# The last megabyte of a weight stream, moved as 114 and 14 partitions

## What is computed

```python
h = x + (merged @ p['w_o']).astype(x.dtype)
h = h + moe(rmsnorm(h, p['norm2_w']), ...)
# moe, for a block of tokens xblk of expert e:
gl = jnp.minimum(xblk @ w_gate[e] + b_gate[e], SWIGLU_LIMIT)
ul = jnp.clip(xblk @ w_up[e] + b_up[e], -SWIGLU_LIMIT, SWIGLU_LIMIT)
return ((ul + 1.0) * (gl * jax.nn.sigmoid(SWIGLU_ALPHA * gl))) @ w_down[e] + b_down[e]
...
y_prompt = rmsnorm(hp, final_norm_w)
y_sample = rmsnorm(hs, final_norm_w)
```

## Time and profile before

| | us |
|---|---|
| median of 3 runs | 1409.24 |
| lowest and highest | 1408.97, 1410.02 |
| the profiled execution, its own time | 1409.07 |
| its span, first to last instruction | 1407.3 |
| TensorE busy | 1340.0 (95%) |
| VectorE busy | 461.4 (33%) |
| ScalarE busy | 230.9 (16%) |
| DMA, mean over the span | 323 GB/s |

### The profile page before, as it was taken

One profiled execution on the slowest core, in us unless ns is written; L12 is line 12 of the kernel. 1 busy time (PEld: TensorE's weight loads), 2 busy tenths in 40 slices (PEclk: granted clock), 3 DMA queues, 4 the chain that ended last, 5 costly groups with the idle time before them and its releaser, 6 DMA issues.

```text
span 1407.3 us, 16551 instructions
## 1 busy us (share of the span) xinstructions
PE 1340.0 (95%) x7269; PEld 671.8 (48%) x7269; DVE 461.4 (33%) x866; ACT 230.9 (16%) x468; POOL 0.2 (0%) x4
## 2 busy tenths in 40 slices
PE   7999999999999999999999999899999999999996
PEld 4556677655554543443434434344343443434432
DVE  3565254263112432232232222313223232232233
ACT  4344231230001110110111101011010110101112
POOL 0000000000000000000000000000000000000000
PEclk9999999999999999999999999999999999999998
DMA  9343331011814899999999999999999999999994
GB/s 340 127 127 132 120 69 62 1 61 60 306 65 187 342 425 428 432 431 430 431 431 431 430 432 431 431 432 430 431 432 429 432 431 429 432 431 430 424 428 187
DMA packets 57179, 455.21 MB, mean 323 GB/s; under 512 B 12820, under 2 KB 24377, under 8 KB 42384
## 3 DMA queue, kind: packets, MB, share of 16 engines
q1 hardware_dynamic: 56960, 454.05, 78.0%
q10 hardware_dynamic: 144, 0.07, 0.0%
HBM read 449.46 MB, written 4.64 MB: 323 GB/s over the span
## 4 chain that ended last, share of the span: by engine, by line
PE 72%; DMA 23%; DVE 3%; ACT 1%; issue 0%; ACTq 0%; SPq 0%; DVEq 0%
PE ps L1120 32%; DMA sb_ring<-in_w_up_dram 20%; PE ps L789 9%; PE ps L596 9%; PE ps L1096 6%; PE ps L1015 3%; PE ps L803 3%; PE ps L569 3%; DMA sb_ring<-in_w_down_dram 2%; PE ps L638 1%; PE ps L1156 1%; DVE sb_xg L2080 1%; PE ps L884 1%; PE ps L1179 1%; PE ps L894 0%; DVE sb_h L2151 0%
## 5 line engine op out<-in xcount | busy, mean ns | idle before, releaser
L1120 PE MATMUL ps<-sb_ring,sb_xg 128*64 128x512 f32 x2048 | 456.6, 599 | 30.1 <-DMA sb_ring<-in_w_up_dram 24.7
L1120 PEld LDWEIGHTS ps<-sb_ring,sb_xg 128*64 128x64 f32 x2048 | 142.2, 137 | 298.2 <-issue 258.1
L1120 PE MATMUL ps<-sb_ring,sb_hidT 128*64 128x512 f32 x992 | 219.0, 594 | 2.8 <-DMA sb_ring<-in_w_down_dram 2.7
L1120 PEld LDWEIGHTS ps<-sb_ring,sb_hidT 128*64 128x64 f32 x992 | 72.4, 137 | 135.9 <-issue 135.0
L789 PE MATMUL ps<-sb_xn,sb_ring 128*128 128x384 f32 x384 | 132.6, 491 | 0.0
L596 PE MATMUL ps<-sb_xn,sb_ring 128*128 128x384 f32 x384 | 126.3, 487 | 1.3 <-DVE sb_xn L1711 1.3
L2113 DVE TENSOR_TENSOR sb_hg<-ps,sb_biases 128x512 f32<-128x512 f32 x32 | 22.1, 691 | 288.4 <-PE ps L569 288.4
L596 PEld LDWEIGHTS ps<-sb_xn,sb_ring 128*128 128x128 f32 x384 | 72.2, 190 | 50.5 <-DVE sb_xn L1711 1.5
L789 PEld LDWEIGHTS ps<-sb_xn,sb_ring 128*128 128x128 f32 x384 | 71.1, 190 | 48.8 <-issue 3.6
L2151 DVE TENSOR_TENSOR sb_h<-sb_h,ps 128x512 f32<-128x512 f32 x90 | 56.5, 683 | 105.4 <-PE ps L1156 105.3
L1096 PEld LDWEIGHTS ps<-sb_onehot,sb_xn 128*128 128x128 f32 x720 | 81.5, 192 | 12.2 <-issue 12.2
(11 more groups left out here) (325 smaller groups left out, 1049.5 us busy)
## 6 DMA issues: line engine op xcount, KB each, us to landing
sb_ring<-in_w_down_dram SPq DMA_DIRECT2D x26, 4096.0 KB, 28.0
sb_ring<-in_w_up_dram SPq DMA_DIRECT2D x26, 4096.0 KB, 30.7
sb_ring<-in_w_gate_dram SPq DMA_DIRECT2D x25, 4096.0 KB, 31.7
sb_ring<-in_w_gate_dram SPq DMA_DIRECT2D x14, 2048.0 KB, 15.5
sb_ring<-in_w_up_dram SPq DMA_DIRECT2D x12, 2048.0 KB, 15.0
sb_ring<-in_w_in_dram SPq DMA_DIRECT2D x11, 2048.0 KB, 9.8
sb_ring<-in_w_down_dram SPq DMA_DIRECT2D x11, 2048.0 KB, 17.6
sb_ring<-in_w_br_dram SPq DMA_DIRECT2D x2, 2048.0 KB, 8.2
```

Of the source, the lines that this page charges most:

```text
L1120: last = mm(o, x(k), columns(kind, w, i, j), start=(k == 0), stop=(k == KT8 - 1))
```

## The change

The second column block of the last half, 1 MB for 128 partitions, is no longer one transfer. It is issued as two transfers, one for partitions 0 to 113 (`LAST_ROWS = 114`) and one for partitions 114 to 127. Both count on `loaded[5]`, and TensorE waits for 16 more on it. The bytes, their places and everything else stay.

```diff
+        LAST_ROWS = 114
...
             sp_.wait_ge(S["used"], q - 6)
-            for c, signal in enumerate((piece_in[(q + 1) % 8], loaded[5])):
-                block = slice(512 * c, 512 * c + 512)
-                dma(slot(q + 1).rearrange("p (t n) -> p t n", t=4)[:, :, block], wd[E - 1, :, 4:8, block]).then_inc(signal, 16)
+            last = slot(q + 1).rearrange("p (t n) -> p t n", t=4)
+            dma(last[:, :, 0:512], wd[E - 1, :, 4:8, 0:512]).then_inc(piece_in[(q + 1) % 8], 16)
+            for rows in (slice(0, LAST_ROWS), slice(LAST_ROWS, P)):
+                dma(last[rows, :, 512:1024], wd[E - 1, rows, 4:8, 512:1024]).then_inc(loaded[5], 16)
...
-            pe.wait_ge(loaded[5], 16 * (TRUNK_SLOT.count(5) + 1))
+            pe.wait_ge(loaded[5], 16 * (TRUNK_SLOT.count(5) + 2))
```

## The result

The kernel with the cut transfer takes 1413.54 us against 1409.24 us (medians of 7 runs each; 1411.38 to 1416.21 against 1407.48 to 1411.05). The ratio is 1.0033 with an interval of 1.0023 to 1.0042: 3 to 6 us slower. I had forecast 1409.3 and no change. The profiled execution took 1412.47 us, 3.40 more than the profiled one before.

The account below looks back on a forecast made before the run. The weight stream was taken to set the pace, with late piece q heading the final chain. Terms summed to 0 to +0.7 us, leaning to +0.1: 1409.2 against the profiled 1409.07, 1409.3 for the median; range 1408.4 to 1411.6.

Parts of the forecast that it names:

- What bounds the kernel, and the slack of 3.5 us: Weight stream sets the pace; piece q, the last down matrix's first half, is late; the block lies ready 3.5 us early.
- 114 rows go to six engines: In the cut transfer, six DMA engines take 19 rows each, up to 20 with the second part, instead of 8.
- The divisor rule: A transfer's rows are dealt evenly to as many DMA engines, up to 16, as divide their number.
- The price of a row: At the stream's end, 12 more rows per engine at 24.4 GB/s take 4.0 us more; block lands by 1392.9.
- The other bound of the prediction: For the cut block, 14.4 GB/s per engine: 8.7 us more, hidden from the early group, +5.3 us from the latest engine.
- the two odd stores: Stores of 3 and 24 rows in the profile before, where 5.3 engines moved 14.4 GB/s each.
- The rival of contention: At the stream's end, six engines disturb the late ones bringing piece q: 2.4 us, 1411.7; chance 0.12.
- a late engine among the six: Rival at the cut block: the latest engine takes its rows, landing at 1392.9, +0.7 us, 1409.9; chance 0.28.
- The extra issue: On SP, a third issue of 0.38 or another 6.6 us ends by 1368, with 24 us of cover: 0 us.
- The range: 1408.4 to 1411.6 us for the whole kernel, to hold 8 in 10; few engines and the slow late engine left out.
- the joint case: At the stream's end, contention with the late engine also among the six and staying slow: +5.3 us, 1414.6.
- the bound that was given 5 in 100: Contention at 14.4 GB/s per engine costing over 2.8 us, the block landing after 1395.0; chance 0.05.

Follow-up runs that it names:

- 122 + 6: Block cut into 122 and 6 partitions instead of the change's 114 and 14; 1421.66 us, ratio 1.0089 to the kernel before.
- 112 + 16: Block cut into 112 and 16 partitions instead of the change's 114 and 14; 1412.7 us, ratio 1.0030 to the kernel before.
- 120 + 8: Block cut into 120 and 8 partitions instead of the change's 114 and 14; 1413.59 us, ratio 1.0028 to the kernel before.
- 64 + 64: Block cut into two halves of 64 partitions instead of the change's 114 and 14; 1412.55 us, ratio 1.0039 to the kernel before.
- the table of four: Against the kernel before, written/read: even-odd/even-odd 0.9998, halves/even-odd 1.0030, even-odd/halves 1.0006, halves/halves 1.0039.
- the held kernel: The change, but SP issues both transfers of the block only when piece q has landed; 1409.7 us, ratio 1.0009 to the kernel before.
- the filled kernel: The change, plus three unused matmuls just before TensorE's wait for piece q; 1414.22 us, ratio 1.0030 to the kernel before.
- its crossed version: Block written to partition halves 0-63 and 64-127 but read from even, then odd rows, instead of the change's cut; 1413.49 us, ratio 1.0030 to before.
- half a dose: Instead of the change: tiles 0-1 of the block in one 128-partition transfer, tiles 2-3 cut 114 + 14; 1411.33 us, ratio 1.0018 to before.
- the last kernel: The kernel before, with piece q cut by columns into two transfers of 128 partitions; 1408.43 us, ratio 0.9997 to the kernel before.

## Why the prediction was wrong, step by step

- **What bounds the kernel, and the slack of 3.5 us.** Right as a reading of the kernel before. Wrong was to treat it as fixed: the change moved the landing of piece q, which the forecast left untouched because it is ahead in the queues. Being ahead in the queues did not protect it: the wait for it was 2.4 to 4.1 us in the profiles of the cuts at 64, 112, 114 and 120, against 1.3.
- **114 rows go to six engines.** The divisor rule is borne out by 122 + 6, where the share is that of two engines, and whose +12.7 us lies in the 7 to 15 worked out from it. In "DMA: Bandwidth & Descriptors", section "Why a DMA increments its semaphore by 16 and not by 1", the Trainium skill gives that rule; the 0.13 x 16 = 2.1 engines agree.
- **The price of a row: "I take the rate of the stream's own end", 24.4 GB/s.** This is the step that failed. At that rate the block was to land by 1392.9 at the latest; it landed at 1395.65. Measured per engine at work: 13.3 GB/s in the change, 13.5 to 14.3 in the cuts 64, 112 and 120, and 16 to 17 for the last two engines of the change. The forecast took nothing off for engines that disturb one another and gave that 0.12. The other bound of the prediction, 14.4 GB/s from the two odd stores, has the size that was measured. That is partly luck: they go the other way, out of SBUF, and no run shows that they are slow for the same reason. 24.4 was right for the six engines issued after piece q, which moved 23.5 each.
- **The rival of contention.** Its mechanism is what happened. Its size was off: it gave 2.4 us for a disturbed piece q and 5.3 us with a late engine among the six, with 0.12 of the chance. Measured is +4.3 us (median), between the two. In the profiled execution piece q is 1.47 us later, not 2.4, and the block lands 6.8 us later, not 8.7. What it lacked was the clock: +1.70 us on 24 matmuls after 2.38 us of idle time. In the change that term can't be added to the block's: with the clock kept up nothing was gained, since the block itself was not there. In 112 + 16, 120 + 8 and 64 + 64, where the block was there, the longer wait and the slower matmuls together are 3.6, 4.4 and 3.2 us, against medians of +3.7, +4.6 and +3.8.
- **The extra issue at 0 us.** Right in effect, wrong in length: the issue of the 14 rows was held 22.5 us (the row of line 527 below), far over the 6.6 us that I took. It ended at 1381.7, and SP had nothing else to do until the outputs, which hid it all. The cut by tiles shows that one transfer more costs nothing.

```profile
L527 SPq DMA_DIRECT2D sb_ring<-in_w_down_dram x2: 4281/13374/22466, 1354.9 to 1359.3; - x2
```

- **The range.** Its upper end of 1411.6 left out the joint case, contention with a late engine. The 13.3 GB/s of the change are nearer to the bound that was given 5 in 100 than to the rate of the forecast.

What is shown: the place written to decides (the table of four), an even load does not help (112 + 16), the harm is gone when the block comes after piece q (the held kernel), and the idle time halves the clock (the filled kernel). Argued only: why. Total rates of 218 to 251 GB/s with 16 engines at work, some 0.5 to 0.6 of 424, look as if two engines met at one way into SBUF at a time. "SBUF — State Buffer", section "SBUF: two separate sides", in the Trainium skill says that DMA engines can contend where several write to one AXI port; the rates fit. Which partitions an engine of a 128-partition transfer serves is not in a trace. That the even and odd cut is free fits engines that serve neighbouring partitions in both; it does not prove it. For 64 + 64 and its crossed version there is a rival that no run here separates: a part of 64 neighbouring partitions may reach fewer ways in, whichever engine writes. The cuts at 112 and 120 are as slow with nearly all partitions in one part, so it can't be the whole. It stays open, too, why half a dose disturbed piece q as much as a whole one in its profile.

## What to carry to other kernels

Cut a transfer by columns or tiles and keep all 128 partitions in each part, above all at the end of a saturated stream: cuts at 64, 112, 114 and 120 partitions cost 3 to 5 us here, the cuts by tiles or into even and odd partitions none that could be told. An even load is no protection. When you cost a transfer that is dealt out in a new way, don't take the stream's rate as given: work it out with half that rate as well, and let it slow what runs beside it, also what stands ahead of it in the queue; then ask whether the new idle time of TensorE brings its clock down.

## What the runs showed of the hardware that I had not expected

- Two partition cuts with the same bytes and the same number of rows in each part (even and odd, and 64 + 64) differ by a factor of 1.8 in rate, by the partitions they write to: 24.7 against 13.5 GB/s per engine.
- In these profiles an idle time of 1.3 us left TensorE's clock at 2.4 GHz; idle times of 2.4 to 4.1 us were followed by a stretch at 1.2 GHz, in which the same 24 matmuls took 6.7 to 7.1 us instead of 5.4.
- An issue near the end of the stream can hold SP for long: 22.5 us behind the 114 rows in the change, but also 17.7 us in the last kernel, in which every transfer there has all 128 partitions. In the cuts by tiles, into halves and into even and odd partitions it was 6.6 to 9.1 us. What sets it stays open.
